# Second block's values projected in two halves of 512 columns, copy-outs of queries and keys moved one piece ahead, and the output projection's tiles issued in halves beside steps 11 to 18

## What is computed

```python
def second_block(x, g_pre_mix, g_post_mix, w_qkv, w_o, rel_bias, g_pre_ffn, g_post_ffn, w_gate, w_up, w_down):
    for i in range(DEPTH):
        h = rms_norm_2(x, g_pre_mix[i])
        m = chunk_relpos_attention(h, w_qkv[i], w_o[i], rel_bias[i // N_MIXERS])
        x = x + rms_norm_2(m, g_post_mix[i])
        h = rms_norm_2(x, g_pre_ffn[i])
        x = x + rms_norm_2(swiglu(h, w_gate[i], w_up[i], w_down[i]), g_post_ffn[i])
    return x
```

## Time and profile before

| what | value |
|---|---|
| time, median of 3 runs | 772.55 us (771.13 to 773.19) |
| profiled execution, its own time | 772.04 us |
| its span from first to last instruction | 770.3 us |
| PE busy | 733.5 us (95%) |
| DVE / ACT busy | 418.9 us (54%) / 337.9 us (44%) |
| mean granted TensorE clock | 0.993 |
| second block's projections, attention and output projection | 469.6 to 576.4 us of the span |

### The profile page before, as it was taken

The page is one execution under the profiler, slowest core; times in us unless marked ns, Lnnn a source line. Parts: engine busy times, 40 slices in busy tenths (PEclk is TensorE's granted clock), DMA queues, the critical chain, the costliest instruction groups (busy, mean ns, idle before and its releaser), DMA issues.

```text
span 770.3 us, 12515 instructions
## 1 busy us (share of the span) xinstructions
PE 733.5 (95%) x5170; PEld 605.9 (79%) x5170; DVE 418.9 (54%) x738; ACT 337.9 (44%) x604; POOL 32.1 (4%) x64
## 2 busy tenths in 40 slices
PE   8999999999999999999887789999999999999997
PEld 8998988888888866666556449999878888888885
DVE  5667756667666521111010118676668767777676
ACT  6866565554444421111010127565656444444443
POOL 1700000000000000000000001000001000000001
PEclk9999999999999999999999999999999999999999
DMA  9953667347988999999999998953334554545101
GB/s 342 416 216 115 220 216 284 124 163 290 361 325 339 367 390 423 421 419 420 421 420 421 413 418 338 419 191 130 146 109 164 185 198 166 208 172 202 73 1 55
DMA packets 33018, 206.07 MB, mean 268 GB/s; under 512 B 3904, under 2 KB 4288, under 8 KB 11200
## 3 DMA queue, kind: packets, MB, share of 16 engines
q1 hardware_dynamic: 32960, 205.25, 68.8%
HBM read 204.18 MB, written 1.05 MB: 266 GB/s over the span
## 4 chain that ended last, share of the span: by engine, by line
PE 85%; DMA 11%; ACT 1%; issue 1%; DVE 1%; SPq 0%; DVEq 0%; POOLq 0%; POOL 0%; ACTq 0%
PE ps L700 45%; PE ps L770 11%; DMA gb<-in_w_down_e 7%; PE ps L773 5%; PE ps L1099 4%; DMA X<-in_w_down_e 4%; PE ps L1120 3%; PE ps L1130 2%; PE ps L1023 1%; PE ps L810 1%; PE ps L1246 1%; PE ps L1220 1%; PE ps L1260 1%; PE ps L1274 1%; DMA raw<-in_dense 1%
## 5 line engine op out<-in xcount | busy, mean ns | idle before, releaser
L1826 DVE TENSOR_TENSOR wl<-raw,wh 128x1024 fp32r<-128x1024 f32 (+3 forms) x181 | 213.0, 1194 | 129.1 <-ACT wh L1409 128.0
L1409 ACT CAST wh<-raw 128x1024 fp32r<-128x1024 f32 (+3 forms) x181 | 181.7, 1024 | 68.4 <-PE ps L700 45.3
L700 PE MATMUL ps<-wh,fra 128*128 128x512 f32 (+3 forms) x636 | 179.1, 367 | 0.0
L700 PEld LDWEIGHTS ps<-wh,fra 128*128 128x128 f32 x636 | 112.9, 189 | 17.4 <-issue 1.0
L700 PE MATMUL ps<-wl,fra 128*128 128x512 f32 (+3 forms) x318 | 115.1, 362 | 0.0
L770 PE MATMUL ps<-fra,wh 128*128 128x512 f32 x352 | 110.7, 396 | 0.7 <-DVE fra L1837 0.7
L773 PEld LDWEIGHTS ps<-fra,wl 128*128 128x128 f32 x352 | 66.1, 188 | 15.5
L700 PE MATMUL ps<-wh,frb 128*128 128x512 f32 x240 | 74.3, 391 | 0.0
L773 PE MATMUL ps<-fra,wl 128*128 128x256 f32 x352 | 69.2, 278 | 0.0
L700 PE MATMUL ps<-fra,wh 128*128 128x256 f32 x368 | 67.9, 286 | 0.0
L700 PEld LDWEIGHTS ps<-wl,fra 128*128 128x128 f32 x318 | 59.9, 188 | 9.0
(11 more groups left out here) (291 smaller groups left out, 1010.2 us busy)
## 6 DMA issues: line engine op xcount, KB each, us to landing
raw<-in_dense SPq DMA_DIRECT2D x79, 1024.0 KB, 5.4
ext<-in_w_down_e SPq DMA_DIRECT2D x20, 1024.0 KB, 18.4
raw<-in_w_gate_e SPq DMA_DIRECT2D x17, 1024.0 KB, 23.8
ext<-in_w_up_e SPq DMA_DIRECT2D x14, 1024.0 KB, 21.4
big<-in_w_up_e SPq DMA_DIRECT2D x8, 1024.0 KB, 18.1
big<-in_w_gate_e SPq DMA_DIRECT2D x7, 1024.0 KB, 27.0
raw<-in_dense SPq DMA_DIRECT2D x13, 512.0 KB, 5.7
raw<-in_w_up_e SPq DMA_DIRECT2D x6, 1024.0 KB, 20.6
```

Of the source, the lines that this page charges most:

```text
L700: t = e.matmul(o, a, w, start=first and n == 0, stop=final and n == 2, skip_group_check=not check)
L1409: e.copy(halves(q)[0], piece_view(q)).then_inc(*up("wh", q))
L1826: e.tensor_tensor(l, piece_view(q), h.bitcast(F), ALU.subtract).then_inc(*up("wl", q))
```

## The change

The values are cut into two halves of 512 columns (`("v", 0)` and `("v", 1)`), each of four pieces with two rows of 512 columns, 12 matmuls of 512 columns for a piece. The new order `QKV` is q0 k0 v0 q1 k1 q2 k2 q3 k3 v1, the same 24 pieces and the same number and sizes of loads. q0, k0 and v0 come ahead of the attention, which leaves 16 pieces of fill instead of 18. DVE's `keep_q` and `keep_k` stand directly behind the last piece's part of the stream instead of one piece later. `keep_v` copies 512 columns at a time: half 0 at the start of the fill, half 1 when the fill is exhausted, in ACT's step 11. DVE issues two pieces of v0 ahead of the copy of the row of factors. On PE `HALVES_AT` takes the place of `TILE_AT`: half tiles (k, i), from step 11 on.

```diff
-FILL_B = (1, 2, 1, 2) * 3
+FILL_B = (1, 1, 2, 1, 2, 1, 1, 2, 1, 2, 1, 0)
+HALVES_AT = {11: ((0, 0),), 12: ((0, 1), (1, 0)), 13: ((1, 1), (2, 0)), 14: ((2, 1), (3, 0)), 15: ((3, 1), (4, 0)), 16: ((4, 1),),
+             17: ((5, 0),), 18: ((6, 0),)}
+QKV = (("q", 0), ("k", 0), ("v", 0), ("q", 1), ("k", 1), ("q", 2), ("k", 2), ("q", 3), ("k", 3), ("v", 1))
...
-    for c in range(4):
-        for n, key in enumerate("qkv"):
-            col = 1024 * n + 256 * c
-            w = tiles(a["w_qkv_2"][0])[:, :, col:col + 256]
-            wt.split((key, c), *((w[:, 0:4], w[:, 4:8]) if (key, c) == ("q", 0) else (w,)))
+    qkv = tiles(a["w_qkv_2"][0])
+    for key, c in QKV:
+        if key == "v":
+            w = qkv[:, :, 2048 + 512 * c:2560 + 512 * c]
+            wt.split((key, c), w[:, 0:4], w[:, 4:8])
+        else:
...
+        def projected(key, c):
+
+            if key == "v":
+                return tokens((key, c), 1, hT, ("kept v2", c))
+            return features((key, c), "qk".index(key), hT, ("kept " + key, c))
+
+        def later_projections():
+            for key, c in QKV[3:]:
+                yield from projected(key, c)
...
-            if k % 2 == 0:
-                e.wait_ge(*at("kept v2", k // 2, 1))
+            if k % 4 == 0:
+                e.wait_ge(*at("kept v2", k // 4, 1))
...
-            if step in TILE_AT:
-                o_tile(TILE_AT[step], *([((0, 0), (0, 1))] if step > 16 else []))
+            for k, i in HALVES_AT.get(step, ()):
+                o_tile(k, ((i, 0), (i, 1)))
...
-                e.activation(H[:, i, 256 * c:256 * c + 256], bank[2 + i][:, 0:256], ACT.Copy, scale=rr[:, i:i + 1]).then_inc(
+                e.activation(H[:, i, 512 * c:512 * c + 512], bank[2 + i][:, :], ACT.Copy, scale=rr[:, i:i + 1]).then_inc(
...
-        def other_quarters():
-            for c in range(1, 4):
-                queries = stream(("q", c))
-                yield next(queries)
-                keep_v(c - 1)
-                yield from queries
-                yield from stream(("k", c))
-                yield from stream(("v", c))
-            keep_v(3)
+        def later_projections():
+            keep_v(0)
+            yield from stream(QKV[3])
+            for key in QKV[4:]:
+                yield from stream(key)
+            keep_v(1)
...
-        def other_quarters():
-            for c in range(1, 4):
-                yield from stream(("q", c))
-                for key, keep in (("k", keep_q), ("v", keep_k)):
-                    pieces = stream((key, c))
-                    yield next(pieces)
-                    keep(c)
-                    yield from pieces
+        def later_projections():
+            for key, c in QKV[3:9]:
+                yield from stream((key, c))
+                (keep_q if key == "q" else keep_k)(c)
+            yield from stream(QKV[9])
...
+        first = stream(("v", 0))
+        next(first)
+        next(first)
         spread_row("krow", 6)
...
-        whole(stream(("v", 0)))
-        fill = other_quarters()
+        whole(first)
+        fill = later_projections()
```

More of the change, by code:

```diff
@@ L251, in weights @@
     wt.expert_end = len(wt.units)
-    for c in range(4):
-        for n, key in enumerate("qkv"):
-            col = 1024 * n + 256 * c
-            w = tiles(a["w_qkv_2"][0])[:, :, col:col + 256]
-            wt.split((key, c), *((w[:, 0:4], w[:, 4:8]) if (key, c) == ("q", 0) else (w,)))
+    qkv = tiles(a["w_qkv_2"][0])
[4 more added lines that the diff above has]
+        else:
+            col = 1024 * "qk".index(key) + 256 * c
+            w = qkv[:, :, col:col + 256]
+            wt.split((key, c), *((w[:, 0:4], w[:, 4:8]) if c == 0 and key == "q" else (w,)))
     for k in range(0, 8, 2):
@@ L1223, in first_queries @@
                 t.then_inc(*up("piece", q))
[L1225 to L1230, removed]
-        def other_quarters():
-            for c in range(1, 4):
-                yield from quarter(c)
+        def projected(key, c):
[5 more added lines that the diff above has]
+                yield from projected(key, c)
         def r_scores(k):
@@ L1305, in tensor @@
         turn_back(1)
-        whole(quarter(0))
+        whole(projected("k", 0))
+        whole(projected("v", 0))
         spread("krow", 6)
-        fill = other_quarters()
+        fill = later_projections()
         next(fill)
```

## The result

| | before | changed |
|---|---|---|
| median of 22 runs each | 772.18 us (769.93 to 776.42) | 773.95 us (772.46 to 776.06) |
| profiled execution, its own time | 772.04 us | 774.07 us |
| its span | 770.3 us | 771.7 us |
| PE matmuls | 5170 | 5074 |

The ratio is 1.0022 (95% interval 1.0013 to 1.0030): the changed kernel is 1.7 us slower (1.0 to 2.3), within 0.3%. A second comparison of 12 runs gave 1.0013 (1.0003 to 1.0023). The forecast had +0.4 us.

A forecast was written before the change was run, and what follows sets the result against it. PE's own work was taken to bound the stretch, with no waits. Wider values -0.96, a new step 11 wait +1.3 and the attention's start +0.1 summed to +0.4 us: 773.0 us against a 772.55 median, range 770.7 to 774.8.

The forecast's parts named there:

- The bound: From first key piece to last output tile, PE is busy 106.80 of 106.80 us and waits for no other engine.
- Wider values: Eight value pieces on PE, each 12 matmuls of 512 columns instead of 24 of 256: 0.12 us less each, -0.96 us.
- The wait in step 11: PE's first output tile waits at bank 2 for ACT's copy-out of the last values: +1.3 us (1.2 to 1.6).
- The start of the attention: At head 0's transposes PE arrives 10.9 us after the row of factors, DVE's division at 10.7: +0.1 us (0 to 0.5).
- Halves of tiles: Output tiles on PE cut into halves of 6 matmuls in 1.39 us, half of 2.76: cutting costs nothing.
- Copy-outs a piece sooner: DVE's copy-outs of queries and keys, needed as bank 0 is re-entered after two pieces: 0 us, bound 2.9 us.
- The sum: Stretch terms -0.96 + 1.3 + 0.1 = +0.4 us, giving 773.0 us against the median of 772.55.
- the bank would be free in time: Rival: ACT reaches the last values' copy ahead of PE in step 11, so no wait; 771.7 us, chance 0.20.
- Thin steps starving PE: Rival: from step 2, early copy-outs hold DVE and PE waits at transposes, up to 2.9 us; 775.8 us, chance 0.08.
- matmul counts pay by their busy time: Rival: 96 fewer matmuls and weight loads on PE save more than 0.96 us, say 3; 769.5 us, chance 0.03.

The follow-up runs named there:

- the kernel with both moves: Changed kernel with ACT's last values copy-out in step 10 and DVE's seventh subtraction ahead of its wait for GpSimd's factor: stretch 106.29 and 106.28 us, ratios 0.9994 and 0.9989.
- e1: Changed kernel with ACT's copy-out of the last values moved from the end of step 11 to the end of step 10: stretch 106.64 us, ratio to before 0.9996.
- e4: Changed kernel with each 512-column values matmul cut into two of 256 columns, 192 in place of 96: stretch 108.94 us, ratio to before 1.0029.

## Why the prediction came out as it did

- **The bound.** Right: what changed is PE's sum in the stretch and PE's waits, and nothing else was found.
- **Wider values, -0.96 us.** Right in kind, mis-sized: they are worth 1.10 us. The term took a piece's 2.76 us from an output tile behind transposes. In an unbroken row of matmuls the difference is larger (0.63 us for four pieces), and behind scores or values of heads it is smaller. The measured gain with both waits gone, 0.93 us, is near 0.96 because 0.17 us of small costs of the new order stand against it; that is luck.
- **The wait in step 11, +1.3 us.** Right in place, cause and recorded length (1.33 us idle), mis-sized in cost: 1.56 us. The working came to 1.24 and was put down as 1.3. PE's arrival at 1.03 us of the step was added up from lengths in the chain of waits, in which a busy matmul runs past the start of the next; PE was due at 546.86, 0.86 us after 546.00. The copy was done a little later than the 2.27 us of the working (0.68 us long, near the 0.65 taken), and PE went on at 2.36. Starting again cost another 0.07.
- **The start of the attention, +0.1 us.** The size was near and the row was not. Head 0 is divided 497.67 - 487.04 = 10.6 us after the row of factors (10.7 forecast), and its transposes don't wait. What waits 0.2 us on PE's weight loads are the scores of step 2, for head 1's mask (`p_maximum`): banks 4 and 5 are entered again there. The step is lengthened by 0.06 us.
- **Halves of tiles, 0.** "Cutting costs nothing" is 0.07 us off, most of it in one place: in the chain of the kernel with both moves the halves of steps 11 and 16 take 1.41 and 1.60 us, 3.01 together, where one whole tile takes 2.95 at step 16 before.
- **Copy-outs a piece sooner, 0.** Right against the new order as it stands; the bound of 2.9 us was far too wide, since leaving them out costs 0.33 us.
- **What was missed, +0.37 us.** The prediction read that PE never waits in the stretch, and worked out no slack for the pieces ahead of the attention. In the kernel before, DVE's subtraction for the seventh piece was 0.51 us ahead of PE; the new order brings PE there 0.65 us sooner. This is the step that failed: each of the pieces that change place should have had its own comparison of when `wl` is done and when PE comes.
- **The sum.** -1.10 + 1.56 + 0.37 + 0.06 + 0.07 = +0.96 us, and +1.00 was measured in the stretch, where +0.4 was forecast. The time's 1.7 us have 1.0 at the lower end of their interval, and the second comparison's 1.0 us match it; the forecast +0.4 lies outside the first interval. That the change would stay within 0.3% came true, but any sum between -2.3 and +2.3 us would have done that, so it says little for the working.
- **The rivals.** That the bank would be free in time is what e1 makes true; in the changed kernel it is false. Thin steps starving PE showed only as tenths (0.06 us in the changed kernel, 0.33 with late copy-outs, 0.42 with whole tiles), never as a piece. That matmul counts pay by their busy time was wrong by e4: 1.10 us for 96 matmuls, not 3.

## What to carry to other kernels

Where the bounding engine never waits, an edit can only save what it takes out of that engine's own work, and each instruction that is then reached sooner has a producer whose spare time must be read first: here a saving of 1.10 us met two producers that were late by 1.5 and 0.2 us and cost 1.56 and 0.37. A short wait can be missing from PE's idle time altogether; it is then seen only at the weight loads and in the chain of waits. To price a change in PE's own work, compare two kernels that have the same waits. When a stage is moved up, look for the first writer of each buffer that the stage before it filled, and move that buffer's copy-out with it. Cutting work into halves for cover pays only if the halves' own buffers are free at the new place.

## What the runs showed of the hardware

- A wait on a PSUM bank cost PE 1.56 us where the profile shows 1.33 idle. 0.17 of the difference is waiting that lies under a matmul of 512 columns, which counts as busy for 0.40 us while the next one starts 0.23 us after it when nothing holds it; 0.07 is a slower start behind the wait.
- DVE's late subtraction held PE for 0.21 us and cost 0.37, and PE's idle time shows none of it; only the weight loads show a wait, of 0.5 us.
- At a granted clock of 1.00, cutting 96 float32 matmuls of 512 columns into 192 of 256 cost 1.10 us, between 11 and 12 ns for each matmul more. It was 0.63 us for four pieces in an unbroken row and 0.47 for the four between other work.
